# Last stage of a hybrid decoder layer: the weight row multiplied beside the statistic in all groups, and the halves of the last block side by side

## The chip, the cores and the metric

The kernel runs on one Trainium2 chip, on 8 cores with one program. Each core has its own part of the tokens and all weights; the cores don't exchange anything. The metric is the device time in microseconds of the slowest core, as a median of several runs.

## The reference, cut to what matters

One decoder layer is computed for 8 sequences of 2048 tokens and 128 short sequences of 8 tokens, width 1024: a half-step SwiGLU, a mixer (short convolution and chunked gating), a second half-step SwiGLU, and the stage that is changed here, the per-layer input embedding:

```python
def rmsnorm(x, g):
    xf = x.astype(jnp.float32)
    y = xf * lax.rsqrt(jnp.mean(xf * xf, axis=-1, keepdims=True) + EPS)
    return (y * g.astype(jnp.float32)).astype(x.dtype)
...
    # per-layer input embedding
    gate = jax.nn.sigmoid(h @ ple_w_gate)
    h = h + rmsnorm(gate * (p_emb @ ple_w_proj), ple_post_g)
```

`h` has 1024 columns, `p_emb` 256. All inputs are fp32; the matmuls run in bf16.

## The kernel before, in words

A core has 2176 tokens: one prompt sequence of 2048 and 128 tokens of the short sequences. It works in two passes, pass one over nine blocks of 128 tokens and pass two over eight. Each pass goes through all stages of the layer. Weights stream through a ring of eight slots, filled by GpSimd's DMA queue; the residual `h` of a pass stays in the on-chip memory, tokens on partitions. The order of the instructions on each engine is that in which Python writes them. Engines wait for each other by one semaphore an engine (`Eng.wait`, `Eng.mark`); each helper (`act`, `stt`, `tt`) takes the events that it waits for. So every ScalarE instruction has line L219, every VectorE multiply or add of two tensors L227, and every combined one (`stt`: a tensor by a factor per token, then times or plus a tensor) L223.

The last stage of a pass is `ple`. In pass two it takes the eight blocks as groups [0,1], [2,3], [4,5], [6,7]. For each block there are these steps:

- gate: `proj_block`, 16 matmuls of 128x512 (L559) into a pair of PSUM banks; `embed`: 8 matmuls (L862) into another pair. There are four pairs, used in turn, and TensorE waits until the reader of a pair is done.
- `sigmoid` on ScalarE, from PSUM into the block's fp32 buffer `gb(b)`.
- `product` on VectorE: the buffer times the embed result from PSUM.
- `rstd_of` on ScalarE: a square with a sum over the row, then two small activations, logarithm and exponential, that give the factor per token.
- the weight row (`gain`), the factor and the residual are put on by VectorE, and the block is stored from SP's DMA queue (`store`, L870).

Sigmoid stands in one function table of ScalarE, logarithm and exponential in another. The compiler puts an ACT_TABLE_LOAD ahead of an instruction whose function isn't in the loaded table. `table(func)` is a tiny activation on one column, written so that the load comes at that place.

Groups [0,1] and [2,3] end in `finish`: buffer times factor times weight row, in place, then plus `h`, both behind the factor:

```python
            e = stt([e3, gain_ev[base + GPLE]], gb(b), gb(b), r, gain(base + GPLE))
            nxt["stt"] = e
            e = tt([e], gb(b), gb(b), h_t[:, b, :], ALU.add)
```

Group [4,5] goes through `middle_two`: the product times the weight row goes to a buffer of its own (`zg_of`) as soon as the product is there, beside the statistic; behind the factor one combined instruction (times factor, plus `h`) is left. The loads of the tables are placed by `table`.

Group [6,7] goes through `last_two`. Both embeds are done ahead of the gate of block seven, and that gate is computed as two halves of 512 columns. For each half there are a sigmoid, a product, a multiply by the weight row and a square. Block six's logarithm and exponential (`rstd_rest`) stand between the second half's sigmoid and its square. A small copy turns the first half's sum into a bias for block seven's logarithm. Then come the combined instruction of block six and two of block seven, each with its store.

Of the kernel before, what the change touches and what calls it, by code (L numbers as in the profile page):

```python
# [7 lines left out]
AF = mybir.ActivationFunctionType  # L8
ALU = mybir.AluOpType
# [17 lines left out]
G1POST, GMPRE, GMPOST, G2PRE, G2POST, GPLE = range(6)  # L27
# [93 lines left out]
def build_program():  # L121
# [51 lines left out]
    bigf = big_t[:].bitcast(F32)  # L173
# [7 lines left out]
    def gb(b):  # L181
        if b in (4, 5):
            return zsc_t[:, b - 4, :]
        o = 1024 * b if b < 4 else 8192 + 1024 * (b - 6)
        return bigf[:, o:o + 1024]
# [31 lines left out]
    def act(wait, **kw):  # L217
        ACT.wait(wait)
        return ACT.mark(nc.scalar.activation(**kw))  # L219
# [5 lines left out]
    def tt(wait, out, in0, in1, op):  # L225
        DVE.wait(wait)
        return DVE.mark(nc.vector.tensor_tensor(out=out, in0=in0, in1=in1, op=op))  # L227
# [41 lines left out]
    def release(f, ev):  # L269
        slot_rel[f % NSLOT] = ev  # L270
        issue_next()
# [11 lines left out]
    gain_ev = {}  # L283
# [8 lines left out]
    def gain(i):  # L292
        return gain_t[:, i % 3, :]
# [4 lines left out]
    def rstd_of(src, junk, wait, n, c=1.0, stop=False):  # L298
        e = st_n["i"] % 16
        st_n["i"] += 1  # L300
        s = st_t[:, e, :]
        e1 = act(wait, out=junk, in_=src, func=AF.Square, accum_out=s[:, 0:1])
        if stop:
            return s, e1, n, c
        return rstd_rest((s, e1, n, c))

    def rstd_rest(a):
        s, e1, n, c = a
        e2 = act([e1], out=s[:, 1:2], in_=s[:, 0:1], func=AF.Ln, bias=c * EPS, scale=c / n)
        e3 = act([e2], out=s[:, 2:3], in_=s[:, 1:2], func=AF.Exp, scale=-0.5)  # L310
        return s[:, 2:3], e3, e1
# [533 lines left out]
    def ple(P, N, base, pT_ev, groups):  # L845
# [26 lines left out]
        def gate(b, last):  # L872
            pair, gate_ev[b] = proj_block(P, b, 8, lambda k: nT_t[:, k, b * 128:(b + 1) * 128], 4, fg, [nT_ev[b]], last)
            del nT_ev[b]
            return pair

        def sigmoid(b, pair):
            pt, lo, hi = pair
            sig[b] = act([gate_ev[b], gb_guard(b)], out=gb(b), in_=pt[:], func=AF.Sigmoid)
            lo.free = hi.free = sig[b]  # L880

        def product(b, pair, ev):
            pt, lo, hi = pair
            zev[b] = tt([ev, sig[b]], gb(b), pt[:], gb(b), ALU.mult)
            lo.free = hi.free = zev[b]
# [8 lines left out]
                h_free[b] = e  # L894

        def zg_of(b):
            return bigf[:, 4096 + 1024 * (b - 4):4096 + 1024 * (b - 3)]

        def table(func):
            nxt["tab"] = act([nxt.get("tab")], out=sv_t[:, 0, 0, 0:1], in_=ones_t[:, 0:1], func=func)  # L900

        def middle_two(b0, b1):
            for b in (b0, b1):
                sigmoid(b, gate(b, False))
            table(AF.Ln)
            st = {}
            for b in (b0, b1):
                product(b, *embed(b, False))
            for b in (b0, b1):
                st[b] = rstd_of(gb(b), sg_t[:].rearrange("p a s -> p (a s)"), [zev[b]], D)  # L910
                st[b] += (tt([zev[b], gain_ev[base + GPLE]], zg_of(b), gb(b), gain(base + GPLE), ALU.mult),)
            table(AF.Sigmoid)
            for b in (b0, b1):
                r, e3, e1, ez = st[b]
                out_ev[b] = store(b, stt([e3, e1, ez], gb(b), zg_of(b), r, h_t[:, b, :], ALU.mult, ALU.add))

        def last_two(b0, b1):
            zg = [zg_of(b0), zg_of(b1)]
            junk = bigf[:, 10240:10240 + D]
            gp = gain(base + GPLE)  # L920
            q = st_t[:, st_n["i"] % 16, :]
            st_n["i"] += 1
            sigmoid(b0, gate(b0, False))
            e0, e1 = embed(b0, False), embed(b1, True)
            product(b0, *e0)
            r0 = rstd_of(gb(b0), sg_t[:].rearrange("p a s -> p (a s)"), [zev[b0]], D, stop=True)
            z0 = tt([zev[b0], gain_ev[base + GPLE]], zg[0], gb(b0), gp, ALU.mult)
            pt, lo, hi = get_pair()
            pe, plo, phi = e1[0]
            half = []  # L930
            for o, cols in ((lo, slice(0, 512)), (hi, slice(512, D))):
                PE.wait(nT_ev[b1], fg[0][1], fg[1][1])
                ins = None
                for k in range(8):
                    f = fg[k // 4][0]
                    o0 = (k % 4) * 1024 + cols.start
                    ins = nc.tensor.matmul(o.t, nT_t[:, k, b1 * 128:(b1 + 1) * 128],
                                           ring_t[:, f % NSLOT, o0:o0 + 512], start=(k == 0), stop=(k == 7))
                half.append((cols, PE.mark(ins)))
            for f, _ in fg:  # L940
                release(f, half[1][1])
            z1 = []
            sq = []
            for i, (cols, ev) in enumerate(half):
                es = act([ev, gb_guard(b1)], out=gb(b1)[:, cols], in_=pt[:, cols], func=AF.Sigmoid)
                ez = tt([es, e1[1]], gb(b1)[:, cols], pe[:, cols], gb(b1)[:, cols], ALU.mult)
                z1.append(tt([ez], zg[1][:, cols], gb(b1)[:, cols], gp[:, cols], ALU.mult))
                if i == 0:
                    sq.append(act([ez], out=junk[:, cols], in_=gb(b1)[:, cols], func=AF.Square, accum_out=q[:, 0:1]))
                    sq.append(act([sq[0]], out=q[:, 0:1], in_=q[:, 0:1], func=AF.Copy, bias=EPS, scale=1.0 / D))  # L950
                else:
                    r, e3, _ = rstd_rest(r0)
                    sq.append(act([ez], out=junk[:, cols], in_=gb(b1)[:, cols], func=AF.Square, accum_out=q[:, 1:2]))
            lo.free = hi.free = es
            plo.free = phi.free = ez
            e4 = act([sq], out=q[:, 2:3], in_=q[:, 1:2], func=AF.Ln, bias=q[:, 0:1], scale=1.0 / D)
            e5 = act([e4], out=q[:, 3:4], in_=q[:, 2:3], func=AF.Exp, scale=-0.5)
            e = stt([e3, z0], gb(b0), zg[0], r, h_t[:, b0, :], ALU.mult, ALU.add)
            out_ev[b0] = store(b0, e)
            for i, (cols, _) in enumerate(half):  # L960
                e = stt([e5, z1[i]], gb(b1)[:, cols], zg[1][:, cols], q[:, 3:4], h_t[:, b1, cols], ALU.mult, ALU.add)
                out_ev[b1] = store(b1, e, cols)
            nxt["stt"] = e
# [18 lines left out]
        for gi, grp in enumerate(groups):  # L982
            lastg = gi == len(groups) - 1
            if N is None and lastg:
                last_two(*grp)
                break
            if N is None and gi == len(groups) - 2:
                middle_two(*grp)
                continue
            for b in grp:  # L990
                pair = gate(b, lastg and b == grp[-1])
                if N is not None and b == 3:
                    xs["st"] = x_stat(N, 0, xs["sq"], gain(base + NGAIN + GMPRE)[:, 0:512])
                    xt_load(N, 1, 1, [xstat_ev[1, 0], fin])
                sigmoid(b, pair)
            if N is not None and gi == 0:
                xs["sq"] = x_square(N, 0, [guards["zsc"]])
            if N is not None and gi == 1:
                gain_load(base + NGAIN + GMPRE, [x_apply(N, 0, *xs["st"], [gate_ev[3]])])
            for b in grp:  # L1000
                pair, ev = embed(b, lastg and b == grp[-1])
                product(b, pair, ev)
            if N is not None and gi == 0:
                fin = first_three(grp)
                continue
            st = {b: rstd_of(gb(b), sg_t[:].rearrange("p a s -> p (a s)"), [zev[b]], D) for b in grp}
            for b in grp:
                finish(b, st[b])
            if N is not None and not lastg:
                pay_owed(None, NFILL + 2 + gi)  # L1010
# [5 lines left out]
    def gb_guard(b):  # L1016
        if b in (4, 5):
            return [guards["zsc"]]
        return [xn_ev[1, 0][-1]] if b >= 6 and (1, 0) in xn_ev else []
# [36 lines left out]
    for P in PASSES:  # L1056
        base = P.idx * NGAIN
        N = PASSES[P.idx + 1] if P.idx == 0 else None
# [75 lines left out]
        groups = [[0, 1, 2], [3, 4, 5], [6, 7, 8]] if P.nb == 9 else [[0, 1], [2, 3], [4, 5], [6, 7]]  # L1134
# [105 lines left out]
```

How the kernel before makes its waits and increments, by code:

```python
    def wait(self, *evs):  # L62
        best = {}
        for ev in _flat(evs, []):
            if ev.key not in best or best[ev.key].val < ev.val:
                best[ev.key] = ev
        for ev in best.values():
            if self.seen.get(ev.key, 0) >= ev.val:
                continue
            self.e.wait_ge(ev.sem, ev.val)
            self.seen[ev.key] = ev.val
            if _COLLECT is not None and ev.idx is not None:
                _COLLECT.add((ev.key, ev.idx))
# [1 line left out]
    def mark(self, ins):  # L75
        self.idx += 1
        if _USED is not None and (self.name, self.idx) not in _USED:
            return Ev(self.sem, self.n, self.name, self.idx)
        self.n += 1
        ins.then_inc(self.sem, 1)
        return Ev(self.sem, self.n, self.name, self.idx)
# [8 lines left out]
    def add(self, ins):  # L90
        self.n += 16
        ins.then_inc(self.sem, 16)
        return Ev(self.sem, self.n, self.name)
```

## Time and profile before

| | us |
|---|---|
| median of 3 runs | 1310.12 |
| lowest and highest | 1309.73, 1310.42 |
| profiled execution, its own time | 1310.42 |
| its span on the slowest core (core 6) | 1309.4 |
| spans of the 8 cores | 1305.4 to 1309.4 |
| TensorE busy on core 6 | 1282.9 (98%) |
| VectorE busy | 523.4 (40%) |
| ScalarE busy | 418.6 (32%) |

The profile is of one execution. Times in it count from the first instruction of a core to the last. PE is TensorE, DVE is VectorE, ACT is ScalarE, SPq is the queue from which SP issues DMAs. A matmul's end is modelled. A number after the letter L is the line of the kernel, mostly that of a helper. An idle time with an arrow names the engine that ended the wait.

### The profile page before, as it was taken

The numbers are of one execution on the slowest core, as the hardware profiler recorded it, in microseconds if no ns is written. First come the engines' busy times: TensorE is split into PE (matmuls) and PEld (weight loads), VectorE is DVE, ScalarE is ACT, GpSimd is POOL, SyncE is SP. The second block draws the span as 40 slices with busy tenths as digits, with TensorE's granted clock in tenths as the row PEclk, the third lists the DMA queues.
The fourth block names the chain that finished last, engine by engine and source line by source line (L and its number), as shares of the span: only waits on it lengthen the run. The fifth ranks groups of instructions, "written<-read, shape, count | busy, mean of one in ns | idle before, by whom it ended". The sixth has DMA issues, their size and how long they took to land.

```text
span 1309.4 us, 18733 instructions; the slowest of 8 cores (1305.4 to 1309.4 us)
## 1 busy us (share of the span) xinstructions
PE 1282.9 (98%) x6734; PEld 651.5 (50%) x6816; DVE 523.4 (40%) x694; ACT 418.6 (32%) x870; POOL 94.6 (7%) x185
## 2 busy tenths in 40 slices
PE   8999999999999999999999999999999999999996
PEld 6566654455545666654444444444444444444442
DVE  3322223347697222222357321124467821212247
ACT  3311112344456111111168111123344811111137
POOL 2100000001001100000001100000010020000000
PEclk9999999999999999999999999999999999999998
DMA  9999322129625973231189996321396299333123
GB/s 214 173 213 216 66 49 49 29 42 179 117 48 90 178 130 65 49 65 33 28 176 257 219 200 113 62 49 25 76 170 117 57 159 171 65 66 56 33 41 129
DMA packets 88474, 139.89 MB, mean 107 GB/s; under 512 B 58304, under 2 KB 58560, under 8 KB 87872
## 3 DMA queue, kind: packets, MB, share of 16 engines
q0 software_dynamic: 25296, 90.25, 41.5%
q1 hardware_dynamic: 63088, 48.43, 13.7%
q8 instruction: 57, 0.93, 0.3%
q14 instruction: 33, 0.27, 0.1%
HBM read 206.03 MB, written 9.51 MB: 165 GB/s over the span
## 4 chain that ended last, share of the span: by engine, by line
PE 91%; ACT 3%; DVE 2%; issue 2%; DMA 2%; SPq 0%; ACTq 0%; DVEq 0%
PE ps L214 59%; PE ps L559 27%; PE ps L548 3%; DMA h<-xT 1%; PE ps L862 1%; ACT L219 1%; DVE big L223 1%; DVE big L227 1%; DVE nT L223 1%; PE ps L711 1%; ACT sg L219 1%; PE ps L502 0%; DMA nT<-nbr 0%; ACT big L219 0%; PE ps L807 0%
## 5 line engine op out<-in xcount | busy, mean ns | idle before, releaser
L214 PE MATMUL ps<-nT,ring 128*128 128x384 bf16 (+1 forms) x4127 | 768.7, 347 | 3.6 <-DMA nT<-nbr 1.1
L214 PEld LDWEIGHTS ps<-nT,ring 128*128 128x128 bf16 x4160 | 407.1, 98 | 361.1 <-issue 5.1
L227 DVE TENSOR_TENSOR big<-ps,sg 128x384 bf16<-128x384 f32 (+1 forms) x220 | 133.7, 610 | 464.7 <-PE ps L214 457.8
L559 PE MATMUL ps<-ring,big 128*128 128x512 bf16 x1291 | 283.7, 379 | 1.5
L219 ACT ACTIVATE sg<-ps 128x384 f32<-128x384 f32 (+1 forms) x237 | 126.5, 537 | 481.2 <-PE ps L214 477.5
L559 PEld LDWEIGHTS ps<-ring,big 128*128 128x128 bf16 x1320 | 129.2, 98 | 155.5
L255 POOL DMA_DIRECT2D ring<-w x170 | 90.2, 539 | 1043.6 <-PE ps L214 410.4
L219 ACT ACTIVATE big<-ps 128x1024 bf16<-128x1024 f32 (+4 forms) x89 | 75.3, 862 | 224.0 <-PE ps L559 192.9
L227 DVE TENSOR_TENSOR zsc<-ps,gains 128x1024 f32<-128x1024 f32 x51 | 62.3, 1222 | 180.6 <-ACT big L219 180.5
L559 PE MATMUL ps<-ring,nT 128*128 128x512 bf16 x470 | 104.7, 379 | 0.9 <-issue 0.4
L559 PEld LDWEIGHTS ps<-ring,nT 128*128 128x128 bf16 x480 | 46.8, 98 | 57.1 <-issue 1.3
L223 DVE SCALAR_TENSOR_TENSOR h<-zsc,st,h 128x1024 f32<-128x1024 f32 x51 | 65.5, 1285 | 11.1 <-DVE zsc L227 6.6
L227 DVE TENSOR_TENSOR big<-ps,big 128x384 f32<-128x384 f32 (+3 forms) x78 | 50.4, 679 | 37.3 <-PE ps L214 22.0
L223 DVE SCALAR_TENSOR_TENSOR nbr<-h,st,gains 128x1024 bf16<-128x1024 f32 x34 | 43.6, 1282 | 37.2 <-ACT st L219 37.2
L219 ACT ACTIVATE nbr<-h 128x1024 bf16<-128x1024 f32 x34 | 35.9, 1057 | 46.6 <-DVE h L223 42.0
L219 ACT ACTIVATE st<-st 128x1 f32<-128x1 f32 x205 | 41.7, 203 | 18.5 <-ACT st L219 0.5
L219 ACT ACT_TABLE_LOAD x31 | 39.8, 1283 | 10.8 <-PE ps L559 3.5
L219 ACT ACTIVATE big<-big 128x384 bf16<-128x384 f32 (+3 forms) x46 | 26.4, 605 | 38.7 <-DVE big L227 38.7
L548 PE MATMUL ps<-ring,big 128*128 128x512 bf16 x175 | 38.6, 379 | 0.1
L214 PE MATMUL ps<-ring,nT 128*128 128x512 bf16 x131 | 29.4, 379 | 0.3
L548 PEld LDWEIGHTS ps<-ring,big 128*128 128x128 bf16 x176 | 17.2, 98 | 20.8
L223 DVE SCALAR_TENSOR_TENSOR nT<-big,gc,zsc 128x384 bf16<-128x384 f32 (+1 forms) x40 | 23.9, 666 | 2.2 <-ACT zsc L219 2.2
(78 smaller groups left out, 366.4 us busy)
## 6 DMA issues: line engine op xcount, KB each, us to landing
ring<-w POOLq DMA_DIRECT2D x170, 512.0 KB, 15.0
h<-x SPq DMA_DIRECT2D x17, 512.0 KB, 36.9
gains<-gain SPq DMA_DIRECT2D x12, 512.0 KB, 11.2
y<-big SPq DMA_DIRECT2D x12, 512.0 KB, 11.5
big<-xT SPq DMA_DIRECT2D x2, 2048.0 KB, 14.5
h<-xT SPq DMA_DIRECT2D x2, 1536.0 KB, 13.1
y<-zsc SPq DMA_DIRECT2D x4, 512.0 KB, 6.7
h<-xT SPq DMA_DIRECT2D x2, 768.0 KB, 7.6
```

Of the source, the lines that this page charges most:

```text
L214: ins = nc.tensor.matmul(out_ap, l, r, start=(i == 0), stop=(i == n - 1))
L219: return ACT.mark(nc.scalar.activation(**kw))
L223: return DVE.mark(nc.vector.scalar_tensor_tensor(out=out, in0=in0, scalar=scalar, in1=in1, op0=op0, op1=op1))
L227: return DVE.mark(nc.vector.tensor_tensor(out=out, in0=in0, in1=in1, op=op))
L255: nc.gpsimd.dma_start(out=ring_t[:, s, o:o + HALF], in_=w_d[f % NFILL, :, o:o + HALF])))
L548: ins = nc.tensor.matmul(o.t, lhs(k), sv[:, k % per, half * 512:half * 512 + 512], start=(k == 0), stop=(k == nk - 1))
L559: ins = nc.tensor.matmul(o.t, lhs(k), sv, start=(k == 0), stop=(k == nk - 1))
L711: ins = nc.tensor.matmul(bank.t[:, 0:w], ones_t[:], sq[i][:, 0:w], start=(c == 0), stop=(c == 3))
L862: ins = nc.tensor.matmul(o.t, pT_v[:, k, b * 128:(b + 1) * 128], sv, start=(k == 0), stop=(k == 1))
```

## The change

In pass two all of the first three groups go through what was `middle_two`, now named `two`. `zg_of` therefore takes its buffer by the block's number modulo four. In `last_two` the work on block seven's halves is put in another order: both sigmoids, then a `table(AF.Ln)` and block six's `rstd_rest`, then on VectorE both products and both multiplies by the weight row, and on ScalarE both squares, with the small copy between them. Pass one is as it was. The small copy now stands behind a logarithm and an exponential and no longer behind a sigmoid.

```diff
         def zg_of(b):
-            return bigf[:, 4096 + 1024 * (b - 4):4096 + 1024 * (b - 3)]
+            return bigf[:, 4096 + 1024 * (b % 4):4096 + 1024 * (b % 4) + 1024]
...
-        def middle_two(b0, b1):
+        def two(b0, b1):
...
-            for i, (cols, ev) in enumerate(half):
-                es = act([ev, gb_guard(b1)], out=gb(b1)[:, cols], in_=pt[:, cols], func=AF.Sigmoid)
-                ez = tt([es, e1[1]], gb(b1)[:, cols], pe[:, cols], gb(b1)[:, cols], ALU.mult)
-                z1.append(tt([ez], zg[1][:, cols], gb(b1)[:, cols], gp[:, cols], ALU.mult))
+            es = [act([ev, gb_guard(b1)], out=gb(b1)[:, cols], in_=pt[:, cols], func=AF.Sigmoid) for cols, ev in half]
+            table(AF.Ln)
+            r, e3, _ = rstd_rest(r0)
+            ez = []
+            for i, (cols, _) in enumerate(half):
+                ez.append(tt([es[i], e1[1]], gb(b1)[:, cols], pe[:, cols], gb(b1)[:, cols], ALU.mult))
+            for i, (cols, _) in enumerate(half):
+                z1.append(tt([ez[i], gain_ev[base + GPLE]], zg[1][:, cols], gb(b1)[:, cols], gp[:, cols], ALU.mult))
+            for i, (cols, _) in enumerate(half):
+                sq.append(act([ez[i]], out=junk[:, cols], in_=gb(b1)[:, cols], func=AF.Square, accum_out=q[:, i:i + 1]))
                 if i == 0:
-                    sq.append(act([ez], out=junk[:, cols], in_=gb(b1)[:, cols], func=AF.Square, accum_out=q[:, 0:1]))
                     sq.append(act([sq[0]], out=q[:, 0:1], in_=q[:, 0:1], func=AF.Copy, bias=EPS, scale=1.0 / D))
-                else:
-                    r, e3, _ = rstd_rest(r0)
-                    sq.append(act([ez], out=junk[:, cols], in_=gb(b1)[:, cols], func=AF.Square, accum_out=q[:, 1:2]))
...
-            if N is None and gi == len(groups) - 2:
-                middle_two(*grp)
+            if N is None:
+                two(*grp)
                 continue
```

## Rows read from the trace of the kernel before

**Rows 1.** Head of the page: the span and those of all cores.
```profile
span 1309.4 us, 18733 instructions; the slowest of 8 cores (1305.4 to 1309.4 us)
```
**Rows 2.** Windows, core 6: length, busy us of PE, PEld, DVE, ACT, POOL, clock, DMA share, GB/s.
```profile
1297.30:1309.40 12.10, 0.00 (x0) 0.00 (x0) 7.26 (x9) 5.84 (x14) 0.00 (x0) 0.69 0.34 134
```
**Rows 3.** Timeline of PE: start, us, instruction; the gates of the groups.
```profile
1271.13 6.85 PE L559 MATMUL ps<-ring,nT 128*128 128x512 bf16 x31
...
1279.54 7.07 PE L559 MATMUL ps<-ring,nT 128*128 128x512 bf16 x31
...
1288.49 3.61 PE L559 MATMUL ps<-ring,nT 128*128 128x512 bf16 x16 [0.15 <-issue]
```
**Rows 4.** Timeline of ACT in groups two to four.
```profile
1281.26 1.06 ACT L219 ACTIVATE sg<-big 128x1024 f32<-128x1024 f32 x1 [1.66 <-DVE big L227]
...
1287.21 1.94 ACT L219 ACTIVATE zsc<-ps 128x1024 f32<-128x1024 f32 x2
1289.17 1.28 ACT L219 ACT_TABLE_LOAD   x1
...
1290.74 1.06 ACT L219 ACTIVATE sg<-zsc 128x1024 f32<-128x1024 f32 x1
...
1295.42 0.20 ACT L219 ACTIVATE sv<-ones 128x1 f32<-128x1 bf16 x1
1295.53 1.01 ACT L219 ACTIVATE big<-ps 128x1024 f32<-128x1024 f32 x1
```
**Rows 5.** Timeline of DVE in groups one to three.
```profile
1274.89 1.29 DVE L223 SCALAR_TENSOR_TENSOR big<-big,st,gains 128x1024 f32<-128x1024 f32 x1 [2.15 <-ACT st L219]
...
1279.95 2.35 DVE L227 TENSOR_TENSOR big<-ps,big 128x1024 f32<-128x1024 f32 x2
...
1291.70 2.35 DVE L227 TENSOR_TENSOR big<-zsc,gains 128x1024 f32<-128x1024 f32 x2
1293.97 2.47 DVE L223 SCALAR_TENSOR_TENSOR zsc<-big,st,h 128x1024 f32<-128x1024 f32 x2
```
**Rows 6.** Timeline of ACT, and last of DVE, in the last group.
```profile
1297.96 1.06 ACT L219 ACTIVATE sg<-big 128x1024 f32<-128x1024 f32 x1 [1.42 <-DVE big L227]
...
1299.02 0.58 ACT L219 ACTIVATE big<-ps 128x512 f32<-128x512 f32 x1
1300.55 0.63 ACT L219 ACTIVATE big<-big 128x512 f32<-128x512 f32 x1 [0.95 <-DVE big L227]
...
1301.36 0.20 ACT L219 ACTIVATE st<-st 128x1 f32<-128x1 f32 x1
...
1302.07 1.28 ACT L219 ACT_TABLE_LOAD   x1
...
1303.77 0.61 ACT L219 ACTIVATE big<-big 128x512 f32<-128x512 f32 x1
...
1304.56 0.59 ACT L219 ACTIVATE st<-st 128x1 f32<-128x1 f32 x2
...
1305.25 1.41 DVE L223 SCALAR_TENSOR_TENSOR big<-big,st,h 128x512 f32<-128x512 f32 x2
```
**Rows 7.** Issues of stores on SP's queue, and the landing of those in the stage.
```profile
1287.07 0.33 SPq L870 DMA_DIRECT2D y<-big  x1
...
1305.32 1.75 SPq L870 DMA_DIRECT2D y<-big  x3
...
DMA to landing us min/median/max: 2.5/2.6/2.7
```
**Rows 8.** Windows of a quarter microsecond, core 6, columns as in the second group.
```profile
1287.75:1288.00 0.25, 0.25 (x3) 0.10 (x1) 0.25 (x1) 0.25 (x1) 0.00 (x0) 1.00 0.53 213
...
1306.00:1306.25 0.25, 0.00 (x0) 0.00 (x0) 0.25 (x2) 0.00 (x0) 0.00 (x0) 0.50 0.53 213
...
1308.75:1309.00 0.25, 0.00 (x0) 0.00 (x0) 0.00 (x0) 0.00 (x0) 0.00 (x0) 0.50 0.31 107
```
**Rows 9.** Timeline of ACT in the mixer: four copies behind two small activations.
```profile
936.02 2.04 ACT L219 ACTIVATE big<-ps 128x512 f32<-128x512 f32 x4
```

More of the change, by code:

```diff
@@ L943, in last_two @@
             sq = []
-            for i, (cols, ev) in enumerate(half):
-                es = act([ev, gb_guard(b1)], out=gb(b1)[:, cols], in_=pt[:, cols], func=AF.Sigmoid)
-                ez = tt([es, e1[1]], gb(b1)[:, cols], pe[:, cols], gb(b1)[:, cols], ALU.mult)
-                z1.append(tt([ez], zg[1][:, cols], gb(b1)[:, cols], gp[:, cols], ALU.mult))
+            es = [act([ev, gb_guard(b1)], out=gb(b1)[:, cols], in_=pt[:, cols], func=AF.Sigmoid) for cols, ev in half]
[8 more added lines that the diff above has]
+                sq.append(act([ez[i]], out=junk[:, cols], in_=gb(b1)[:, cols], func=AF.Square, accum_out=q[:, i:i + 1]))
                 if i == 0:
-                    sq.append(act([ez], out=junk[:, cols], in_=gb(b1)[:, cols], func=AF.Square, accum_out=q[:, 0:1]))
                     sq.append(act([sq[0]], out=q[:, 0:1], in_=q[:, 0:1], func=AF.Copy, bias=EPS, scale=1.0 / D))
-                else:
-                    r, e3, _ = rstd_rest(r0)
-                    sq.append(act([ez], out=junk[:, cols], in_=gb(b1)[:, cols], func=AF.Square, accum_out=q[:, 1:2]))
-            lo.free = hi.free = es
-            plo.free = phi.free = ez
+            lo.free = hi.free = es[1]
+            plo.free = phi.free = ez[1]
             e4 = act([sq], out=q[:, 2:3], in_=q[:, 1:2], func=AF.Ln, bias=q[:, 0:1], scale=1.0 / D)
```

## Prediction

> **What bounds the kernel now.** I read the page's head first: the slowest core needs 1309.4 us, the fastest 1305.4 [rows 1]. The changed stage comes at the end of every core, so a saving in it should be seen on every core. The windows of the stage come next: TensorE is busy until 1297.3, and 12.1 us follow in which it does nothing [rows 2]. All that the change can win lies in those 12.1 us. Only what shortens the way from TensorE's last products to the last store counts.
>
> The timeline of ScalarE (ACT) shows why that way is long. A sigmoid needs one function table and the logarithm another, and each change is a load of 1.28 us. The last matmul of gate six ended near 1292.1 (1288.49 + 3.61 [rows 3]), yet the sigmoid of block six starts at 1295.53 [rows 4]. ScalarE is late by 3.4 us. It is late since the sigmoid of block four, which starts at 1287.21 although gate four had long ended. Before that it had idled 1.66 us until 1281.26, waiting for VectorE's product of block two, which started at 1279.95 [rows 4, 5]. Embed two had ended near 1278.8; VectorE was still busy with the multiply and add pairs of blocks zero and one, which began at 1274.89 after an idle time of 2.15 us for the factor [rows 5]. So the chain goes back from the end along ScalarE to a VectorE that is too late in the second group.
>
> **Groups one and two (blocks 0 to 3).** Six full-width VectorE instructions a group stay six. The two multiplies by the weight row (1291.70 to 1293.97 is 2.27 for two) no longer wait for the factor and go into the idle 2.15 us. In group one that idle time began at 1274.89 - 2.15 = 1272.7, with the products' end. The multiplies run from there to 1274.9, the two combined instructions (2.47 for two, the row at 1293.97) to 1277.4, and VectorE is free then in place of 1279.95 [rows 5]. The factors come from ScalarE by 1273.6 and 1275.3: the table load now stands ahead of the first square, so the first factor comes about 1.1 us earlier and is not waited for. The added tiny activations cost 0.11 each (1295.42 to 1295.53 [rows 4]); the loads are as many as before, two a group, at other places.
>
> Group two: gate three ends at 1271.13 + 6.85 = 1277.98 [rows 3], its sigmoid runs 1278.07 to 1279.09, and load and tiny activation put ScalarE at 1280.51 (0.02 + 1.29 + 0.11 from [rows 4]). Embed two ends at 1278.84; product two then runs 1279.0 to 1280.24, in time. From the first square of such a pair to the next sigmoid the third group shows 1290.74 to 1295.53 = 4.79 [rows 4]. Sigmoid four thus starts at 1285.30 and ends at 1286.32.
>
> **Group three.** Its code is the same; its bound changes. Gate five ends at 1279.54 + 7.07 = 1286.61 [rows 3], later than sigmoid four. So sigmoid five waits for TensorE and starts at 1286.70. Before, the second sigmoid of that pair started at 1287.21 + 1.94 - 1.01 = 1288.14; the load came 1.03 later (1289.17), lasts 1.28, and with 0.01 and the tiny activation's 0.11 the first square could come 2.43 us after the sigmoid's start. That gives 1289.14; before, the square came at 1290.74, when product four had ended [rows 4]. Product four (embed four ends at 1287.47) is done by 1288.95, so it doesn't hold the square. Then the same 4.79: **sigmoid six at 1293.93 in place of 1295.53, 1.60 us earlier**. VectorE's six start at 1287.64, its last at 1293.38, and it is free at 1294.6; product six wants it at 1295.04. That slack of 0.4 us is the cover of the four moved multiplies. TensorE's pause of 0.15 us ahead of gate six (it waited for sigmoid four's banks) goes too, off the path: gate seven ends by 1297.3, sigmoid seven's second half wants it at 1297.92.
>
> **The last pair.** Before, from square six (1297.96) to the first combined half of block seven (1305.25), 7.29 us passed [rows 6], start to start: 1.06 to the first half's sigmoid, 1.53 for the round over VectorE to the first half square, 0.81 to the copy, 0.71 over the second half's sigmoid to the load, 1.70 for the load and the factor of block six, 0.79 for the second half square, and 0.69 for the last two small activations and the way to VectorE. Now: 1.06; 0.50 to the second sigmoid (0.58 less the overlap of two full ones, 2 x 1.01 in 1.94 [rows 4]; without it 0.58); then, in another order, the same 0.71, 1.70, 0.81, 0.79 and 0.69, and 0.11 for the tiny activation. The sum is 6.37. The round of 1.53 is gone and 0.61 takes its place: **0.92 us**. The half products hide it: square six is at 1296.36, the first half's sigmoid from 1297.42 to 1298.0, so VectorE starts the halves near 1298.2. At 0.70 apiece (1.41 for two at 1305.25 [rows 6]) both products end by 1299.6, and the half squares come at 1300.3 and 1301.3. All four halves end by 1301.0, and the combined instruction of block six, whose factor is there at 1300.5, by 1302.3 (half of 2.47 and a little), ahead of 1302.73, where the first combined half starts. If that cover of 0.4 us were gone, each 0.1 more would show one for one.
>
> **The stores.** No DMA is added or passed by another on SP's queue, but they spread. Now three are issued from 1305.32 to 1306.74 [rows 7]. The engines move data from 1306.12 (53% of the first quarter) to 1308.83 (31% of the last): 1 MB in 2.71 us, 387 GB/s, so without a pause [rows 8]. A store by itself, issued at 1287.07, begins to move at 1287.87, 0.80 later [rows 7, 8]. After the change store six is issued near 1301.95, 1.5 us ahead of the first half (1303.47); its data are through by 1304.1. The second half, issued at 1304.22 (2.52 earlier), moves 0.80 + 0.67 us later instead of 2.09: **0.62 us**. Between the bounds 0 and 0.67 (a whole 256 KB turn) I take the worked value. The Trainium skill, "DMA: Bandwidth & Descriptors", in the section on the anatomy of one DMA, gives each transfer about 2.0 us fixed plus its bytes at 436 GB/s. By that the last half would land 2.6 us after its issue, as it does now. The trace doesn't agree for 512 KB (3.2 by the rule, 2.6 in [rows 7]).
>
> **Sum.** 1.60 + 0.92 + 0.62 = 3.14 us: span 1309.4 - 3.1 = 1306.3. The profiled execution took 1310.42 with 1.0 us around its span, so 1307.3; the median of the runs lies 0.3 lower at 1310.12, so I forecast **1307.0**, 0.24% less. A difference under 0.2% (2.6 us) can hardly be told from none here, and the forecast is only just past it.
>
> **Rivals.**
> - The last half lands as late after its issue as now, 2.5 to 2.6 us [rows 7]: a fixed share rather than a queue. Gain 2.52, 1307.6, within 0.2%. For it: the landing is 2.6 with and without neighbours. Against: the windows show no pause from the first byte to the last [rows 8]. 0.14.
> - VectorE or a wait takes the place of the idle time in groups one to three, and sigmoid six gains nothing to half: product six wants VectorE with 0.4 us to spare, and each 0.1 beyond is lost. Gain 1.5 to 2.3, 1307.8 to 1308.6, within 0.2%. 0.12.
> - Slower: table loads. The copy between the two half squares stood under the sigmoid's table and now stands under the logarithm's. If each tiny activation and the copy brought loads of their own, group two would have two more and the last pair two: sigmoid five would wait for ScalarE and not for TensorE. With two in group one and two in group two the square of block four comes 4.2 us later than reckoned, a net of +1.0, 1311.2; with the copy's two, 2.6 more, 1313.7. It decides for slower from three added loads on the path (3.84 against 3.14). Against it: in the mixer four copies run in one piece, with no load in or ahead of them, in the stretch behind the norms' factors [rows 9], and the third group has just two loads. 0.03.
> - More than 3.5 us (a shorter wait somewhere that I count full): under 1306.6. 0.06.
>
> **Chances.** The forecast case (1306.6 to 1307.4) holds 0.65. Past 0.2% are the forecast, nearly whole, and the last of the cases above: faster 0.70. Within 0.2%: the first two rivals and a rest, 0.27. Slower 0.03. The range 1306.1 to 1308.1 takes in the forecast, the store rival and the better half of the second; medians of three also move by some 0.35.
>
> **What the profile would show.** Sigmoid six 2 us after gate six's end instead of 3.4; sigmoids four and five no longer back to back, the second released by TensorE; no idle time of VectorE ahead of the first combined instruction of groups one and two; the halves' two sigmoids 0.5 apart, one load behind them, then square, copy, square; first combined half some 5.4 us after TensorE's last matmul, before 8.0; store data with a gap after store six. Wrong it would be if there are more than eight loads in the stage, if the first combined half waits for VectorE, or if the last landing stays 2.6 us behind its issue.

## The result, and the profile after

The changed kernel takes 0.9978 of the time before, with a 95% interval of 0.9971 to 0.9986. The medians are 1308.15 us over 16 runs and 1310.41 us over 16 runs of the kernel before (both hold some disturbed runs; the ratio leaves them out). On the median before of 1310.12 the ratio gives 1307.2 us, where 1307.0 was forecast. The gain is 2.9 us (1.8 to 3.8). The kernel is faster; whether by more or less than 0.2% (2.6 us) the interval leaves open.

Below is the head of the page of the changed kernel: the span and those of all cores. It answers to [rows 1].

```profile
span 1305.5 us, 18747 instructions; the slowest of 8 cores (1302.2 to 1305.5 us)
```

The cores come to the last stage at different times (its first gate starts at 1262.28 in the profile before and at 1261.41 after), so a span by itself mixes that with the change. The better measure is the stage: from the start of its first gate to the end of the span. Before it was 1309.4 - 1262.28 = 47.1 us; over the eight cores 47.1 to 47.7. After it is 1305.5 - 1261.41 = 44.1 us, over the eight cores 44.1 to 44.4. The difference is 3.0 us between the two slowest cores, 2.8 to 3.5 from core to core, and 3.2 between the means of the eight. To compare a time after with one before on the two slowest cores, 0.87 us is to be added to it.

Timeline of TensorE, changed kernel (start, us, instruction), the gates. A piece of 31 or 32 matmuls holds both gates of a group, one of 16 a single gate. (An embed is four matmuls, two halves of two each; the eight named in the description of the kernel are those of a group's two embeds, so embed two is done halfway through such a piece.)

```profile
1261.41 7.07 PE L559 MATMUL ps<-ring,nT 128*128 128x512 bf16 x32
...
1278.68 7.07 PE L559 MATMUL ps<-ring,nT 128*128 128x512 bf16 x31
...
1287.31 3.62 PE L559 MATMUL ps<-ring,nT 128*128 128x512 bf16 x16
...
1292.49 3.62 PE L937 MATMUL ps<-ring,nT 128*128 128x512 bf16 x16
```

Timeline of ScalarE, changed kernel, from sigmoid four to the end:

```profile
1284.43 1.01 ACT L219 ACTIVATE zsc<-ps 128x1024 f32<-128x1024 f32 x1
1285.85 1.02 ACT L219 ACTIVATE zsc<-ps 128x1024 f32<-128x1024 f32 x1 [0.41 <-PE ps L559]
...
1288.29 1.04 ACT L219 ACTIVATE sg<-zsc 128x1024 f32<-128x1024 f32 x1
...
1293.07 1.01 ACT L219 ACTIVATE big<-ps 128x1024 f32<-128x1024 f32 x1
1295.49 1.06 ACT L219 ACTIVATE sg<-big 128x1024 f32<-128x1024 f32 x1 [1.42 <-DVE big L227]
...
1296.55 1.06 ACT L219 ACTIVATE big<-ps 128x512 f32<-128x512 f32 x2
1297.63 1.28 ACT L219 ACT_TABLE_LOAD   x1
...
1299.42 0.61 ACT L219 ACTIVATE big<-big 128x512 f32<-128x512 f32 x1
...
1300.33 0.61 ACT L219 ACTIVATE big<-big 128x512 f32<-128x512 f32 x1
```

In [rows 4] sigmoids four and five were one piece of 1.94 us. Here sigmoid five has an idle time of 0.41 ahead of it, ended by TensorE: the wait for gate five that the forecast put there. Sigmoid six starts at 1293.07, which is 31.66 us after the stage's first gate; before it was 33.25. On all eight cores the two figures are the same within 0.02 us. The last pair shows the two half sigmoids in one piece, one load, and the two half squares 0.91 apart.

Timeline of VectorE, changed kernel:

```profile
1274.07 2.48 DVE L223 SCALAR_TENSOR_TENSOR big<-big,st,h 128x1024 f32<-128x1024 f32 x2
1278.16 2.36 DVE L227 TENSOR_TENSOR big<-ps,big 128x1024 f32<-128x1024 f32 x2 [1.62 <-PE ps L862]
...
1297.30 1.29 DVE L227 TENSOR_TENSOR big<-ps,big 128x512 f32<-128x512 f32 x2 [0.57 <-ACT big L219]
1298.50 1.28 DVE L227 TENSOR_TENSOR big<-big,gains 128x512 f32<-128x512 f32 x2
1299.70 1.28 DVE L223 SCALAR_TENSOR_TENSOR big<-big,st,h 128x1024 f32<-128x1024 f32 x1
1301.89 1.42 DVE L223 SCALAR_TENSOR_TENSOR big<-big,st,h 128x512 f32<-128x512 f32 x2 [0.91 <-ACT st L219]
```

The products of the second group begin as soon as embed two is there (1278.16; VectorE had idled 1.62 us). In [rows 5] it had no pause in front of them. The combined instructions of the first group (1274.07) have no idle time ahead of them any more, where VectorE had waited 2.15 us for the factor. The last row shows VectorE idle for 0.91 us ahead of the first combined half: it was ready, and ScalarE is what ends the way.

The chain that ended last leaves TensorE at another place. In the kernel before it left at 1279.72, at the products of the second group. (There the view names the event that came last, the end of the group's eight embed matmuls. Product two needs only the first four, done near 1278.8; VectorE had no idle time ahead of it, so it was VectorE's own work that held it until 1279.95.) In the changed kernel it is on TensorE to gate seven's end (start, us, what):

```profile
1292.66 3.47 PE ps L937 x16
...
1297.03 0.59 ACT big L219
...
1297.63 1.28 ACT L219
```

The second half's sigmoid starts 0.9 us after TensorE is through. That is what is left above TensorE's floor at this point; 8.5 us follow to the end of the span.

Timeline of SP's queue, changed kernel, the last three stores:

```profile
1301.06 2.65 SPq L870 DMA_DIRECT2D y<-big  x3
```

The line's own view for the two halves' stores, changed kernel:

```profile
DMA to landing us min/median/max: 2.0/2.0/2.0
```

Windows of a quarter microsecond, changed kernel, columns as in [rows 8]:

```profile
1303.25:1303.50 0.25, 0.00 (x0) 0.00 (x0) 0.05 (x1) 0.00 (x0) 0.00 (x0) 0.50 0.02 0
1303.50:1303.75 0.25, 0.00 (x0) 0.00 (x0) 0.00 (x0) 0.00 (x0) 0.00 (x0) 0.50 0.80 303
...
1304.75:1305.00 0.25, 0.00 (x0) 0.00 (x0) 0.00 (x0) 0.00 (x0) 0.00 (x0) 0.50 0.72 271
```

The DMA engines are all but empty (2%) between store six and the halves. The halves land 2.0 us after their issue, against 2.5 to 2.6 before ([rows 7] and [rows 8]). Over the eight cores the last half takes 2.0 to 2.3 us here and took 2.6 to 3.2 before, on average about 0.7 us more.

### The profile page after: what moved, and what is told of

It is laid out like the page before. It is cut to its first block, busy times and chain, and to the rows that moved or that the text cites. A ratio compares the mean times of both kernels' runs of the same rounds, so it can differ in the third digit from the quotient of the medians.

```text
span 1305.5 us, 18747 instructions; the slowest of 8 cores (1302.2 to 1305.5 us)
## 1 busy us (share of the span) xinstructions
PE 1282.0 (98%) x6734; PEld 651.8 (50%) x6816; DVE 522.8 (40%) x694; ACT 418.9 (32%) x875; POOL 94.7 (7%) x185
## 4 chain that ended last, share of the span: by engine, by line
PE 93%; DVE 2%; ACT 2%; DMA 2%; issue 1%; SPq 0%; ACTq 0%; DVEq 0%
PE ps L214 59%; PE ps L559 28%; PE ps L548 3%; PE ps L862 1%; DMA h<-xT 1%; DVE nT L223 1%; PE ps L711 1%; DVE big L223 1%; DMA nT<-nbr 0%; PE ps L502 0%; ACT big L219 0%; PE ps L807 0%; DVE big L227 0%; ACT L219 0%; PE ps L937 0%
## 5 line engine op out<-in xcount | busy, mean ns | idle before, releaser
L559 PEld LDWEIGHTS ps<-ring,nT 128*128 128x128 bf16 x480 | 46.9, 98 | 56.7 <-issue 0.7
```

The lines of the kernel that those rows point to most:

```text
L559: ins = nc.tensor.matmul(o.t, lhs(k), sv, start=(k == 0), stop=(k == nk - 1))
```

## The experiments

Seven kernels ran besides the two of the prediction. "Stage" is the measure from above, on the slowest core. A kernel with no ratio rests on one profile alone. In each of those the starts of sigmoid six and of the first combined half, counted from the first gate, agree within 0.03 us on all eight cores; what differs from core to core is the landing of the last store, by up to 0.5 us.

| kernel | stage us | ratio to before |
|---|---|---|
| before | 47.1 | 1 |
| changed | 44.1 | 0.9978 (0.9971 to 0.9986) |
| groups only | 45.6 | 0.9985 (0.9976 to 0.9994) |
| last pair only | 45.7 | 0.9988 (0.9979 to 0.9998) |
| first group only, with the last pair | 44.9 | |
| second group only, with the last pair | 44.3 | |
| changed, stores together | 45.6 | |
| changed, two loads more | 47.2 | |
| shorter way | 43.1 | 0.9966 (0.9953 to 0.9979) |

**Groups only.** The last pair gets its old order back.

```diff
-            es = [act(..., func=AF.Sigmoid) for cols, ev in half]
-            table(AF.Ln)
-            r, e3, _ = rstd_rest(r0)
...
+            for i, (cols, ev) in enumerate(half):
+                es = act(..., func=AF.Sigmoid)
+                ez = tt(...)
+                z1.append(tt(...))
+                (square and copy, or rstd_rest and square)
```

> Only the groups part of the change: blocks 0 to 3 multiply the weight row beside the statistic, the last pair is in its old order. Theory (three terms): the sigmoid of block six comes 1.6 us earlier against the end of gate six, the last pair takes its old 7.29 us from square six to the first combined half, and the three stores stay together, so the last one still lands 2.6 us behind its issue. From the first gate of the stage to the span's end 47.1 - 1.6 = 45.5 us; time 1.6 us below before, a ratio of 0.9988. Rival (the last pair alone makes the gain): no change, 47.1. Rival (the groups make it all): 44.1.

Measured: stage 45.6 us, a gain of 1.5; ratio 0.9985, clear of 1. Timeline of ScalarE and VectorE of this kernel (its first gate starts at 1262.36):

```profile
1294.00 1.01 ACT L219 ACTIVATE big<-ps 128x1024 f32<-128x1024 f32 x1
1296.43 1.06 ACT L219 ACTIVATE sg<-big 128x1024 f32<-128x1024 f32 x1 [1.42 <-DVE big L227]
...
1302.43 2.71 DVE L223 SCALAR_TENSOR_TENSOR big<-big,st,h 128x1024 f32<-128x1024 f32 x3 [0.32 <-ACT st L219]
```

Sigmoid six comes 31.64 us after the first gate, as in the changed kernel, and the last pair is as long as before: the three combined instructions start 6.00 us after square six, and did so in the old kernel (1303.96 - 1297.96). The stores land 2.7 us after their issue. The groups give the first term alone. Two things moved in them, the weight row and a table load, and this run doesn't tell them apart; the run with the second group alone says more.

**Last pair only.** The condition in `ple` goes back to the third group alone:

```diff
-            if N is None:
+            if N is None and gi == len(groups) - 2:
                 two(*grp)
```

> Only the last pair in its new order; blocks 0 to 3 as before. Theory: the sigmoid of block six 3.4 us behind gate six as before, then 6.4 us from square six to the first combined half where 7.3 stood, and the stores spread, so the last lands 2.1 us behind its issue: 0.9 + 0.6 = 1.5 us, stage 45.6 us, ratio 0.9988. Rival (landing has a fixed length): 0.9 us, stage 46.2. Rival (the last pair makes all of the gain): 44.1.

Measured: stage 45.7, a gain of 1.4; ratio 0.9988. Timeline of ScalarE and VectorE (its first gate starts at 1263.87):

```profile
1297.15 1.01 ACT L219 ACTIVATE big<-ps 128x1024 f32<-128x1024 f32 x1
1299.58 1.06 ACT L219 ACTIVATE sg<-big 128x1024 f32<-128x1024 f32 x1 [1.42 <-DVE big L227]
...
1305.99 1.41 DVE L223 SCALAR_TENSOR_TENSOR big<-big,st,h 128x512 f32<-128x512 f32 x2 [0.92 <-ACT st L219]
```

Sigmoid six is at 33.28 after the first gate, as late as before the change. From square six to the first combined half it takes 6.41 us, and the last half lands 2.0 us after its issue. So the second and third terms are there without the first. The rival that one part makes all of the gain is out for both parts; 1.5 and 1.4 add up to 2.9 of the 3.0. The two ratios overlap, so the split rests on the profiles and not on them.

**Stores together.** The store of block six is issued behind the first combined half:

```diff
-            out_ev[b0] = store(b0, e)
+            e_six = e
             for i, (cols, _) in enumerate(half):
                 e = stt([e5, z1[i]], ...)
+                if i == 0:
+                    SP.wait(e)
+                    out_ev[b0] = store(b0, e_six)
                 out_ev[b1] = store(b1, e, cols)
```

> The changed kernel, but the store of block six waits for the first combined half of block seven, so the three stores are issued within about 0.7 us again. No engine's work changes. Theory (1 MB goes through at 387 GB/s, and the last half queues behind the rest): data move from about 0.8 us behind the first issue for 2.7 us, and the span ends 1.2 us later than in the changed kernel, stage 45.3 in place of 44.1 us. Rival (a store lands a fixed 2.0 to 2.6 us behind its issue): last landing as in the changed kernel, stage 44.1 to 44.2.

Measured: stage 45.6, 1.5 us longer, with the same work on the engines up to and with the combined halves. The issues on SP's queue, and the line's own view for the last store of this kernel:

```profile
1303.45 1.64 SPq L870 DMA_DIRECT2D y<-big  x3
...
L870 SPq DMA_DIRECT2D y<-big x1: 742/742/742, 1304.3 to 1304.3; - x1
...
DMA to landing us min/median/max: 3.3/3.3/3.3
```

Windows of this kernel, at the start and at the end of the data:

```profile
1304.25:1304.50 0.25, 0.00 (x0) 0.00 (x0) 0.00 (x0) 0.00 (x0) 0.00 (x0) 0.50 0.94 377
...
1306.75:1307.00 0.25, 0.00 (x0) 0.00 (x0) 0.00 (x0) 0.00 (x0) 0.00 (x0) 0.50 0.99 369
1307.00:1307.25 0.25, 0.00 (x0) 0.00 (x0) 0.00 (x0) 0.00 (x0) 0.00 (x0) 0.50 0.24 82
```

The same half store lands 3.3 us after its issue here, 2.6 in the kernel before and 2.0 in the changed one, by how much of the other stores' data stands in front of it. The data run from 1304.25 to 1307.06 without a pause, 1 MB in 2.8 us, so the last half is held by the bytes ahead. A fixed landing time would have shown no change. The 1.2 expected became 1.5: the landing makes 1.3 of it, and the last issue, at 1304.3, comes 42.2 us after the first gate (1262.15) in place of 42.0. SP issues three stores in one piece here, and the last took it 0.74 us instead of 0.33; as the engines had data all the while, that longer issue isn't what the landing waited for.

**First group only, second group only.** `two` for blocks 0 and 1 but not 2 and 3, and the other way round:

```diff
-            if N is None:
+            if N is None and gi != 1:    (first group only)
+            if N is None and gi != 0:    (second group only)
```

> The changed kernel, but blocks 2 and 3 are back in the old form; blocks 0 and 1 and the last pair as changed. Theory: VectorE is free for block two's product at once, so square two comes 0.9 us earlier than before the change, the old form of that group then takes its 5.95 us to sigmoid four, sigmoids four and five run back to back, and square four comes 0.9 us earlier than before instead of 1.6: stage 44.8 us (44.1 with both groups, 45.7 with neither). Rival (the second group alone matters, since it is the one that feeds group three): 45.7. Rival (each group half): 44.9.

> The changed kernel, but blocks 0 and 1 are back in the old form; blocks 2 and 3 and the last pair as changed. Theory: block two's product still starts late, when VectorE is through with the pairs of blocks 0 and 1, so square two comes as late as before the change (0.75 us later than in the changed kernel); the group's new form then gives 4.8 us to sigmoid four. Sigmoid five misses gate five's end by 0.3 us only, and square four comes 1.3 us earlier than before instead of 1.6: stage 44.4 us. Together with the run of the first group alone: 0.9 and 1.3 don't add up to 1.6, because TensorE's gate five is a floor. Rival (shares add): 44.1 + what the first group alone gained.

Measured: 44.9 and 44.3. Against the last pair alone (45.7) the first group by itself gains 0.8 us, the second 1.4, both together 1.6. They don't add up. 44.9 is also what the rival of equal shares said for the first group; the second group's 44.3 rules it out, and the rival that the shares add, too (44.1 + 0.8 = 44.9). At sigmoid six, where the landing of the stores doesn't count, the first group alone gains 0.9 us (32.34 after the first gate, 33.25 before the change) and the second 1.4 (31.88).

Timeline of ScalarE with the first group alone (its first gate starts at 1266.37); sigmoids four and five are one piece, 24.02 after the gate, and were so at 24.93 before the change:

```profile
1290.39 1.94 ACT L219 ACTIVATE zsc<-ps 128x1024 f32<-128x1024 f32 x2
...
1298.71 1.01 ACT L219 ACTIVATE big<-ps 128x1024 f32<-128x1024 f32 x1
```

The timeline of ScalarE and VectorE with the second group alone shows both halves of the reason (its first gate starts at 1265.66):

```profile
1283.33 2.35 DVE L227 TENSOR_TENSOR big<-ps,big 128x1024 f32<-128x1024 f32 x2
...
1283.00 1.28 ACT L219 ACT_TABLE_LOAD   x1
...
1284.64 1.06 ACT L219 ACTIVATE sg<-big 128x1024 f32<-128x1024 f32 x1
...
1289.43 1.92 ACT L219 ACTIVATE zsc<-ps 128x1024 f32<-128x1024 f32 x2
```

Without the first group's new form the product of block two has no idle time in front and starts 17.67 us after the first gate, as before the change (1279.95 - 1262.28). The new form of the second group then takes 4.79 us to sigmoid four instead of 5.95, and sigmoids four and five are one piece again. What the second group can't gain by itself is the last 0.2 us down to gate five's end (31.88 against 31.66 at sigmoid six; 0.3 was expected).

Where do the 4.79 in place of 5.95 come from? Not from the multiplies. In neither kernel does ScalarE wait for VectorE between square two and sigmoid four. What differs there is one table load. In the old form the load for the logarithm stood behind square two, on the way. Timeline of ScalarE, kernel before:

```profile
1282.48 1.28 ACT L219 ACT_TABLE_LOAD   x1
```

In the new form `table(AF.Ln)` puts it ahead of square two (1283.00 above), into the time in which ScalarE waits for the product anyway. One load of 1.28 us is off the way and a tiny activation of 0.11 has come onto it; measured it is 1.16 us (5.95 - 4.79).

So the first term could be the loads' work more than the weight row's, and no run separates the two. An estimate from the rows: in the changed kernel the first group's first factor is done at 1272.75 (1273.6 on the old clock) instead of 1274.7, since no load stands between square and logarithm. The four old instructions of VectorE took 5.06 us (1274.89 to 1279.95). Started at 1273.8, 0.17 behind that factor, they would end at 1278.86, in time for product two at 1279.03. By this estimate the placing of the loads alone would give nearly the whole first term. The weight row alone would free VectorE in time for product two, but leave the load on the way; by the same rows that gives some 0.9 us, as the first group alone did. A kernel with the new loads and the old `finish` would decide it; it wasn't run.

**Two loads more.** At the end of the second group alone, ahead of `table(AF.Sigmoid)`:

```diff
+            if b0 == 2:
+                table(AF.Sigmoid)
+                table(AF.Ln)
             table(AF.Sigmoid)
```

> The changed kernel with two table loads and two tiny activations more at the end of the second group (to the sigmoid's table, back and again), 2 x 1.40 = 2.8 us on ScalarE ahead of sigmoid four. Theory: in the changed kernel sigmoid five waits for gate five, with 0.5 us to spare for ScalarE, so the span ends 2.8 - 0.5 = 2.3 us later: stage 46.4 us, and sigmoids four and five run back to back. Rival (ScalarE's own chain is the bound through group three, as before the change): 2.8 later, 46.9. Rival (ScalarE isn't on the way at all): 44.1.

Measured: stage 47.2. Timeline of ScalarE (first gate at 1265.04):

```profile
1286.65 1.28 ACT L219 ACT_TABLE_LOAD   x1
1287.94 0.20 ACT L219 ACTIVATE sv<-ones 128x1 f32<-128x1 bf16 x1
1288.22 1.28 ACT L219 ACT_TABLE_LOAD   x1
...
1291.20 1.92 ACT L219 ACTIVATE zsc<-ps 128x1024 f32<-128x1024 f32 x2
...
1299.32 1.01 ACT L219 ACTIVATE big<-ps 128x1024 f32<-128x1024 f32 x1
```

The total is above 46.4 and above the rival's 46.9, and by itself it decides nothing: with the price that the loads turn out to have, the rival's total is 47.2 as well. The rows decide. A load with its tiny activation cost 1.57 us here (1288.22 - 1286.65), not 1.40, because the next load starts only when the tiny one is through (1287.94 + 0.20, load at 1288.22). The two delay sigmoid four by 3.14 us (26.16 after the first gate, 23.02 in the changed kernel) and sigmoid six by 2.62 (34.28 against 31.66). The difference of 0.5 us is the spare time ahead of gate five's end; by the rival sigmoid six would have come 3.14 later. Sigmoids four and five run in one piece again, as the theory said. The last store is issued 2.6 us later too. The remaining 0.4 us stand behind it: both halves land 2.5 us after their issue, not 2.0, with the engines 7% and 4% busy in the two last quarters of a microsecond with data. On all cores of this run the last half takes 2.4 to 2.5 us, though store six is as far ahead of it as in the changed kernel (2.0 to 2.3); why stays open.

**Shorter way.** Built from what the others showed. In `two` both squares run one behind the other, each with its own scrap buffer; one logarithm and one exponential serve both blocks; no tiny activation stands ahead of the group's next sigmoid. In `last_two` the first half's sigmoid comes ahead of square six, the load is left to the logarithm, and the copy stands behind both half squares:

```diff
-                st[b] = rstd_of(gb(b), ..., [zev[b]], D)
+                e1.append(act([zev[b]], out=junk[i], in_=gb(b), func=AF.Square, accum_out=q[:, i:i + 1]))
...
-            table(AF.Sigmoid)
+            e2 = act(e1, out=q[:, 2:4], in_=q[:, 0:2], func=AF.Ln, bias=EPS, scale=1.0 / D)
+            e3 = act([e2], out=q[:, 2:4], in_=q[:, 2:4], func=AF.Exp, scale=-0.5)
...
+            half_sigmoid(0)
             r0 = rstd_of(gb(b0), ..., [zev[b0]], D, stop=True)
             z0 = tt(...)
+            half_gain(0)
+            half_sigmoid(1)
+            half_gain(1)
-            table(AF.Ln)
             r, e3, _ = rstd_rest(r0)
```

> The changed kernel shortened where the theory puts the way: both squares of a group one behind the other with a buffer of their own each, one logarithm and one exponential for both blocks, no tiny activation ahead of the sigmoids; in the last pair the first half's sigmoid in ScalarE's idle time ahead of square six, both half squares in one piece and the small copy behind them. Theory: in group three 4.8 us from square four to sigmoid six become 4.1, sigmoid seven's second half then waits for TensorE (0.7 us earlier than in the changed kernel), and square to square goes from 0.92 to 0.62; the tiny activation's 0.1 goes. Sum 1.0 us below the changed kernel, stage 43.1 us, ratio to before 0.9968. Rival (VectorE is the bound in the changed kernel): no more than 0.2 us below it.

Measured: stage 43.1, ratio 0.9966. Timeline of ScalarE (first gate at 1261.45):

```profile
1292.41 1.02 ACT L219 ACTIVATE big<-ps 128x1024 f32<-128x1024 f32 x1
1294.52 0.60 ACT L219 ACTIVATE big<-ps 128x512 f32<-128x512 f32 x1 [1.08 <-PE ps L939]
1295.07 1.06 ACT L219 ACTIVATE sg<-big 128x1024 f32<-128x1024 f32 x1
...
1296.24 0.60 ACT L219 ACTIVATE big<-ps 128x512 f32<-128x512 f32 x1
1296.86 1.28 ACT L219 ACT_TABLE_LOAD   x1
```

Sigmoid six is at 30.96 after the first gate (31.66 in the changed kernel) and the second half's sigmoid at 34.79 (about 35.6). The stage is shorter than the changed kernel's by 1.0 us, as expected, where the rival allowed 0.2: VectorE, which has as many columns to work through as before, wasn't the bound of the changed kernel. The two ratios come from separate series of runs and their intervals overlap a little, so that step rests on the profiles.

## Why the prediction was right

- **The place of the bound.** It put the chain on ScalarE back to a VectorE that is late in the second group. The run with the second group alone shows this: with blocks 0 and 1 in the old form, product two starts as late as ever. But the larger part of the gain doesn't hang on it. That run still gains 1.4 of the 1.6 us, 1.16 of them by the table load that has left ScalarE's way between square two and sigmoid four. The forecast had this in its 4.79 and in the factor that comes 1.1 us earlier, without saying how much the load's place makes. How much the multiplies add to it is not shown.
- **First term, 1.60.** Measured 1.59 in the changed kernel (33.25 - 31.66), and 1.61 with the groups alone (33.25 - 31.64). The steps came out too: on the old clock sigmoids four and five at 1285.30 and 1286.72, square four at 1289.16, and product six 0.37 us behind VectorE's last work, where a slack of 0.4 was forecast. Its limit, gate five's end, is shown by the 0.41 us wait of sigmoid five and by the 0.5 us of the two added loads that had no effect. Product two, forecast at 1279.0 on the old clock, came at 1279.03.
- **Second term, 0.92.** From square six to the first combined half: 1301.89 - 1295.49 = 6.40 against the 6.37 of the sum; the gain was 0.89. The half products were hidden, with more room than reckoned: VectorE idled 0.91 us, where the forecast left 0.4. The half pairs ran at 0.60 an instruction (two in 1.29, the next pair 1.20 after) and I had taken 0.70.
- **Third term, 0.62.** The last half landed 2.0 us after its issue against 2.6. The stage gained 3.0 in all, so 0.5 to 0.6 came from there; as a mean of the eight cores it is about 0.7. The run with the stores together, in which the engines' work is the same, shows that the bytes in front are a cause. They aren't the only one: with store six through, the last half took 2.0 to 2.3 us over the cores of the changed kernel and 2.4 to 2.5 with two loads more, at the same spacing of the stores. The size of this term, to a tenth, is in part luck. The rule of the Trainium skill, "DMA: Bandwidth & Descriptors", in its section on the anatomy of one DMA (2.0 us fixed plus the bytes at 436 GB/s, from which 2.6 us is an estimate for a half), is given there for DMAs of GpSimd, and these stores are SP's. It matches the half of the kernel before, which stood behind other stores, and not that of the changed one: the half alone took 2.0.
- **The slower rival.** The added tiny activations brought no loads of their own: the stage has eight loads before and after, and the copy under the logarithm's table (between the two half squares) has none beside it.
- **What was off.** The first combined half was to come 5.4 us after TensorE's last matmul and came 5.8 us after it (1301.89 - 1296.11). The half wasn't late; TensorE was early. Counted from the first gate it ends 0.3 us sooner than before (34.70 against 35.01), where only its pause of 0.15 was to go. This is off the path and changes no term.
- **The total.** 3.14 forecast, 3.0 seen in the profile of the slowest cores, 3.2 as a mean over the cores, 2.9 by the ratio. The forecast gave 0.70 to more than 0.2%. Sign and size were right; the measured 0.22% can't be told from that 0.2%, so this part stays open.

## What to carry to other kernels

Where the end of a kernel hangs on one engine, follow that engine back to where it first fell behind; here that was two groups earlier. The gain stopped at the next floor (TensorE's gate), which an exact sum from start-to-start times foretold to 0.1 us. Work that needs no result of a wait belongs in front of it. Here that is shown for the table load, which moved into a wait of ScalarE and took 1.16 us off the way; that the multiplies by the weight row had to move as well is not shown, so try the two apart. Spread the last stores: a store queues behind the bytes issued just ahead of it, and half a microsecond at the end is as good as half a microsecond of computing.

## What I had not expected of the hardware

- A load with its tiny activation costs 1.57 us and not 1.40 when another load follows: the second load starts 0.28 after the tiny activation's start, when that is through, where an ordinary activation that doesn't need its result follows 0.11 after it.
- The same 256 KB store landed 2.0, 2.6 or 3.3 us after its issue on the slowest core by what was ahead of it in the queue. With the 512 KB ahead of it through and the stores as far apart as in the changed kernel, it took 2.0 to 2.5 over cores and runs, while the engines' part of the stage agreed within 0.03 us on all cores.
